# A fused encoder layer on one core: the forget gates' functions at the ends of two pairs, and chained sums in ada's first blocks

## The chip, the cores and the metric

The kernel runs on one NeuronCore of a Trainium2 chip. The metric is the device time of one execution in microseconds. A core has five engines with queues of their own: TensorE (PE, with its weight loads shown as PEld), VectorE (DVE), ScalarE (ACT), GpSimd (POOL) and SyncE (SP). They wait for one another by semaphores. Each engine executes its queue in order, so an instruction that waits holds back all that stand behind it.

## What is computed

One layer of a streaming encoder on x (512 tokens, 1024 channels, float32), with a conditioning vector c. Cut to what the change touches:

```python
mod = silu(c) @ ada_w + ada_b                 # 9 x 1024 columns: shift, scale, gate of three sub-layers
h = rms_norm(x) * (1 + sc1) + sh1             # from the first two of the nine
x = x + 0.5 * g1 * swiglu(h, ...)             # FFN 1: 22 x 128 hidden columns
h = rms_norm(x) * (1 + sc2) + sh2
qa, ka, va, fa, qb, kb, vb, ga, gb = split(h @ mix_w_in)
log_f = log_sigmoid(fa + forget_b)            # 8 heads, 512 tokens
F = cumsum(log_f)                             # branch a: logits get F_t - F_s, causal mask
y_b = attention(qb, kb, vb, relative bias)    # branch b: bias by clipped distance, chunk mask
x = x + g2 * (sigmoid(ga) * (y_a @ wa) + sigmoid(gb) * (y_b @ wb)) @ w_out
x = x + 0.5 * g3 * swiglu(...)                # FFN 2, then a last rms_norm
```

## The kernel before, in words

Every product is made of three float32r matmuls (high x high, high x low, low x high; `three`, lines 1489 to 1491). So each weight unit (1024 columns of 128 rows) is loaded by SyncE's queue, copied to a high half by ScalarE (`prep`, line 616) and subtracted to a low half by VectorE (`prep`, line 945). Activations are stored transposed, channels on the partitions.

**Ada's first blocks.** The 1024 shift and 1024 scale columns of the first sub-layer come in four blocks (b = 0 to 3) of 512 columns, each with eight rows of weights a partition (k = 0 to 7), loaded in two halves (`load_first_block`, line 437). A block's sum over the 1024 channels is made in three parts. GpSimd multiplies and adds rows 0 and 1 (`first_rows`, lines 501 to 510, three instructions a block, into `adasp`). VectorE sums the next rows, up to `ROWS_V[b]` (`first_rows`, lines 1071 to 1085, into `adasc`). TensorE multiplies the last rows, those in `ROWS_PE[b]`, by the conditioning itself (`first_parts`, line 1524), and adds `adasp` and `adasc` over the partitions by products with ones (`first_sums`, line 1512). These are matmuls of one column, and the profile counts each float32 one twice. VectorE adds the parts and the bias (`first_columns`, line 1087), scales two tiles of the normalised input (line 1006), ScalarE makes their high half (line 638), VectorE the low half (line 1011). Then TensorE multiplies these two tiles by the first four weight units (`tiles`, in `first_units`, line 1532). The order of TensorE and VectorE is written out by hand: `first_units` mixes `tiles(u, b)`, `first_parts(b)` and `first_sums(b)`; VectorE's `normed` (line 1014) has the rows of block 3 in two pieces around block 2's tiles. `dummies(n)` (line 1613) issues small bf16 matmuls whose result nothing reads.

**The pairs of heads.** Token mixing has two branches. Branch b (relative bias) goes first: `pairs(0)`, four pairs of heads, then `branch(0)`; `pairs(1)` is branch a (forget gates). A pair has five units: queries, keys, values, two gate units. TensorE makes them, the scores of both heads, the transposes of v, then unit 3 (24 matmuls), the transposes of the first head's probabilities (`turn(0)`, line 1822), half of unit 4, the first head's value products (lines 1837 and 1838), and so on. VectorE adds the bias and finds the largest score (`biased_scores`, line 1344), ScalarE takes the exponentials (line 815), VectorE divides (`normalised`, line 1356). The first two pairs of branch b are straight code, `body(0, True)`; the first has its queries, keys and values already made (`made`).

**The forget gates.** ScalarE makes |f| and a rectified part (lines 912 and 913), then in the first pair `forget_exp` (line 774) and `forget_logs` (line 778): Exp, Ln, Exp on 8 partitions x 512. VectorE's `forget_sums` (line 1285), six instructions, stands at the end of the first pair and ends with the running sum. GpSimd then runs, in its queue's order: `biases_b(0)`, `biases_b(1)`, wait for the running sum, write it to memory (line 591), `biases_a(0)` (four broadcasts, line 549, and four masks, line 555), `biases_b(2)`, `biases_b(3)` (a load, line 536, and a mask, line 540), `biases_a(1)` and on. `bias` is one buffer for a pair of branch b, so `biases_b(i)` also waits until the pair before has added its bias; VectorE's first `biased_scores` of pair i waits for `bias_masked` of that pair.

Of the kernel before, what the change touches and what calls it, by code (L numbers as in the profile page):

```python
# [5 lines left out]
ALU = mybir.AluOpType  # L6
# [3 lines left out]
BF16 = mybir.dt.bfloat16  # L10
ds = bass.ds

P = 128
# [5 lines left out]
def hybrid_block(nc, x, c, ada_w, ada_b, norm_ffn1, ffn1_w_gate, ffn1_w_up, ffn1_w_down,  # L19
# [11 lines left out]
    DT = D // P  # L31
# [55 lines left out]
    C_N1, C_NM, C_N2, C_AB, C_GB = 0, DT, 2 * DT, 3 * DT, 3 * DT + N_MOD * DT  # L87
# [8 lines left out]
    ADA0, ADA1, ADA2 = 4, FT // 2 - 1, DT // 2  # L96
# [1 line left out]

    ROWS_P = 2
    ROWS_PE = ((6, 7), (5, 6, 7), (7,), ())
    ROWS_V = [DT - len(rows) for rows in ROWS_PE]

    N_FIRST = 4
    DUMMIES = 44
# [8 lines left out]
    with ctx:  # L115
# [380 lines left out]
        def _(pool):  # L496
# [4 lines left out]
            def first_rows(b):  # L501
                pool.wait_ge(adas_in[b][0], 32)

                nc.gpsimd.tensor_scalar(adasp[:, b, :], adas[:, b, 0, :], csilu[:, 0:1], None, ALU.mult).then_inc(adasp_step, 1)
                for k in range(1, ROWS_P):
                    scaled = sqx[:, 0:AC] if k % 2 else sqx[:, AC:]
                    pool.wait_ge(adasp_step, (b * ROWS_P + k) * 2 - 1 - b)
                    nc.gpsimd.tensor_scalar(scaled, adas[:, b, k, :], csilu[:, k:k + 1], None, ALU.mult).then_inc(adasp_step, 1)
                    pool.wait_ge(adasp_step, (b * ROWS_P + k) * 2 - b)
                    nc.gpsimd.tensor_tensor(adasp[:, b, :], scaled, adasp[:, b, :], ALU.add).then_inc(adasp_step, 1)  # L510

            def relative_table():
# [89 lines left out]
        def _(act):  # L602
# [168 lines left out]
                half_high(2, 0, range(4, DT))  # L771
                half_high(2, 1, range(DT))

            def forget_exp():
                act.wait_ge(fa_act, 1)
                nc.scalar.activation(fgate[:, 1, :], fgate[:, 0, :], ACT.Exp, scale=-1.0).then_inc(fa_act, 1)

            def forget_logs():

                act.wait_ge(fa_act, 2)  # L780
                nc.scalar.activation(fgate[:, 2, :], fgate[:, 1, :], ACT.Ln, bias=1.0).then_inc(fa_act, 1)
                act.wait_ge(fa_act, 3)
                nc.scalar.activation(fgate[:, 4, :], fgate[:, 2, :], ACT.Exp, scale=-1.0).then_inc(fa_act, 1)

            def pairs(br):
                u0 = U_MIX[br]

                def body(i, first=False):
                    for pp in range(2):
# [11 lines left out]
                                    nc.scalar.activation(dst[head_rows(h ^ other), h, :], bank[head_rows(h), k, :], ACT.Copy,  # L801
                                                         scale=sc).then_inc(qhi, 1)
                        if made:
                            forget_exp()
                            prep(u0, 10, i, k0 + 3)
                        act.wait_ge(unit_done, i * 10 + u0 + k0 + 3)
                        nc.scalar.activation(vT[:, :], bank[:, B_V if made else 0, :], ACT.Copy).then_inc(v_copied, 1)
                        if made:
                            forget_logs()
                        prep(u0, 10, i, k0 + 4)  # L810
                        for h in range(2):
                            for n, t in enumerate(T_ORDER):
# [48 lines left out]
                        gate(1)  # L861
                        out_part(1)
                        out_hi(1)

                if br == 0:
                    body(0, True)
# [63 lines left out]
        def _(dve):  # L930
# [83 lines left out]
            def normed():  # L1014
                every = slice(0, SEQ)
                diagonals(0, slice(0, TT))
                first_rows(0, 4, ROWS_V[0])
                first_prep(0)
                first_prep(1)
                dve.wait_ge(bc_done, 1)  # L1020
                dve.wait_ge(xt_done, DT)
                for b in range(DT // 2):
                    if b in (1, 2):
                        first_rows(b, ROWS_P, ROWS_V[b])
                    if b == 1:
                        first_prep(2)
                        first_prep(3)
                    if b == 2:
                        first_rows(3, ROWS_P, 4)
                    if b == 3:  # L1030
                        first_rows(3, 4, ROWS_V[3])
                    first_columns(b)
                    for d in (2 * b, 2 * b + 1):
                        scaled(0, 0, d, every, B_BC[0])
                    for d in (2 * b, 2 * b + 1):
                        low(0, 0, d, every)
# [33 lines left out]

            def first_rows(b, k0, k1):
                acc = bank[:, B_ACC, :]
                done = sum(n - ROWS_P for n in ROWS_V[:b])
                for k in range(k0, k1):
                    if k == k0 or k % 4 == 0:
                        dve.wait_ge(adas_in[b][k // 4], 32)
                    out = adasc[:, b, :] if k == ROWS_V[b] - 1 else acc
                    if k > ROWS_P or b:
                        dve.wait_ge(adas_step, done + k - ROWS_P)
                    if k == ROWS_P:  # L1080
                        ins = V.tensor_scalar(out, adas[:, b, k, :], csilu[:, k:k + 1], None, ALU.mult)
                    else:
                        ins = V.scalar_tensor_tensor(out=out, in0=adas[:, b, k, :], scalar=csilu[:, k:k + 1],
                                                     in1=acc, op0=ALU.mult, op1=ALU.add)
                    ins.then_inc(adas_step, 1)

            def first_columns(b):

                def pick(t, c0, stride):
                    return t[:, c0:c0 + 2 * stride].rearrange("p (a d) -> p a d", a=2)  # L1090
                if b == 0:
# [4 lines left out]
                done = sum(4 if rows else 3 for rows in ROWS_PE[:b])  # L1096
                V.tensor_tensor(out, sums[:, 0], pick(prm, C_AB, DT)[:, :, 2 * b:2 * b + 2], ALU.add).then_inc(mod_first, 1)
                for s in range(1, 3 if ROWS_PE[b] else 2):
# [206 lines left out]
            def pairs(br):  # L1305
                u0 = U_MIX[br]

                def body(i, first=False):
                    for pp in range(2):
# [15 lines left out]
                            V.tensor_tensor(kHL[head_rows(1 - h), h, :], bank[head_rows(h), 1, :], f32(kHL[head_rows(h), h, :]),  # L1325
                                            ALU.subtract).then_inc(d_free[1], 1)
                        prep(u0, 10, i, k0 + 3)
                        prep(u0, 10, i, k0 + 4)

                        def biased_scores(h):  # L1330
                            for n, t in enumerate(T_ORDER):
# [42 lines left out]

                        biased_scores(0)
                        biased_scores(1)
                        normalised(0)
                        dve.wait_ge(vhi, g * 2 + 2)
                        for e in range(2):
# [8 lines left out]
                        prep(u0, 10, i, k0 + 6)  # L1388
                        out_sum(1)
                        out_lo(1)  # L1390
                        if made:
                            forget_sums()

                if br == 0:
# [46 lines left out]
            first_rows(0, ROWS_P, 4)  # L1441
# [42 lines left out]
        def _(pe):  # L1484
# [26 lines left out]

            def first_sums(b):

                for n in range(2 * AC // P):
                    if n == 0:
                        pe.wait_ge(adasp_step, (b + 1) * (2 * ROWS_P - 1))
                    if n == AC // P:
                        pe.wait_ge(adas_step, sum(n_v - ROWS_P for n_v in ROWS_V[:b + 1]))
# [13 lines left out]
            def first_units():  # L1532
# [10 lines left out]

                dummies(20)
                tiles(0, 0)
                tiles(1, 0)
                first_parts(1)
                first_sums(1)
                tiles(2, 0)
                tiles(3, 0)  # L1550
                tiles(0, 1)
                tiles(1, 1)
                tiles(2, 1)
                first_parts(2)
                first_sums(2)
                tiles(3, 1)
                tiles(0, 2)
                tiles(1, 2)
                first_sums(3)
                tiles(2, 2)  # L1560
                tiles(3, 2)
                for u in range(N_FIRST):
                    tiles(u, 3)

# [48 lines left out]
            def dummies(n):  # L1613

                for _ in range(n):
                    T.matmul(bank[:, B_IDLE, 0:2 * P], ident[:, :].bitcast(BF16)[:, 0:P], ident[:, :].bitcast(BF16), start=True, stop=True)  # L1616

            def spread():
                pe.wait_ge(diag_done, 1)
# [360 lines left out]
```

## Time and profile before

| | us |
|---|---|
| median of 3 runs | 1170.51 (1170.43 to 1171.03) |
| the profiled execution | 1172.53 |
| its span, first to last instruction | 1170.8 |
| TensorE busy | 1154.2 |
| VectorE busy | 625.7 |
| ScalarE busy | 451.4 |
| GpSimd busy | 59.1 |

The profiled execution's own time is 1.7 us more than its span, which is what lies around the instructions. Times in the rows are microseconds from the span's start. In a timeline a row gives start, duration, engine, line of the kernel, operation, tiles written and read, shape and count; the brackets at its end say how long the engine was idle before it and whose work ended that. Matmuls overlap, so their durations are longer than the distance between two starts. In a row of a window, each engine has its busy time and its instructions, and the number after GpSimd's is the granted TensorE clock as a share of 2.4 GHz.

### The profile page before, as it was taken

The page shows a single profiled execution, that of the slowest core. Times are in us where ns is not written, and L with a number is a line of the kernel's source. Part 1 is how long each engine was busy: PE and PEld are TensorE (multiplying, and loading weights), DVE is VectorE, ACT ScalarE, POOL GpSimd, SP SyncE. Part 2 cuts the span into 40 slices and gives each one's busy share as a digit, 9 for nine tenths or more (in the row PEclk, how much of TensorE's full clock was granted, in tenths as well). Part 3 has the DMA queues.
Part 4 walks back from the last instruction along what each step waited for, and adds up shares of the span by engine and source line. Part 5 has one row for each costly group of instructions (what it writes and reads, how often), then busy time and mean ns, then how long its engine had stood idle before and what let it go on. Part 6 is the DMA issues. An engine that isn't in the chain of part 4 may idle for free.

```text
span 1170.8 us, 16224 instructions
## 1 busy us (share of the span) xinstructions
PE 1154.2 (99%) x5734; PEld 977.2 (83%) x5734; DVE 625.7 (53%) x1052; ACT 451.4 (39%) x709; POOL 59.1 (5%) x86
## 2 busy tenths in 40 slices
PE   8999999999999998999999999999999999999998
PEld 7788888888888997888888888899888888888887
DVE  4766666666555666765555666756333333333332
ACT  4132232233222355655555666543332222322232
POOL 3301000000000000200000110000000000000000
PEclk9799999999999998999999999999999999999999
DMA  9567666556555413533244442241333333333331
GB/s 313 157 198 245 196 202 211 168 178 224 172 169 164 111 56 90 136 91 90 72 114 96 115 118 87 84 125 47 108 90 94 103 90 101 96 85 99 99 112 73
DMA packets 221149, 151.45 MB, mean 129 GB/s; under 512 B 5078, under 2 KB 202916, under 8 KB 221108
## 3 DMA queue, kind: packets, MB, share of 16 engines
q1 hardware_dynamic: 217108, 138.76, 39.4%
q0 software_dynamic: 3280, 9.79, 3.1%
q10 hardware_dynamic: 720, 2.36, 0.5%
q8 instruction: 25, 0.41, 0.1%
q14 instruction: 16, 0.13, 0.0%
HBM read 148.73 MB, written 4.52 MB: 131 GB/s over the span
## 4 chain that ended last, share of the span: by engine, by line
PE 93%; DVE 2%; issue 2%; DMA 1%; ACT 1%; ACTq 0%; DVEq 0%; POOLq 0%; POOL 0%; SPq 0%
PE bank L1489 28%; PE bank L1491 28%; PE bank L1490 28%; PE bank L1822 2%; PE bank L1838 1%; PE bank L1837 1%; PE bank L1815 1%; PE bank L1810 1%; DMA xin<-in_x_dram 1%; DMA raw<-in_ffn_w_gate_dram 1%; PE bank L1520 1%; DVE hL L1011 1%; PE bank L1616 0%; PE bank L1529 0%; DVE tmp L1006 0%
## 5 line engine op out<-in xcount | busy, mean ns | idle before, releaser
L1489 PE MATMUL bank<-hH,wH 128*128 128x512 f32 (+1 forms) x1072 | 414.3, 386 | 2.6 <-DVE hL L1011 2.2
L1490 PE MATMUL bank<-hL,wH 128*128 128x512 f32 (+1 forms) x1072 | 410.2, 383 | 0.0
L1491 PE MATMUL bank<-hH,wL 128*128 128x512 f32 (+1 forms) x1072 | 410.1, 383 | 0.0
L616 ACT ACTIVATE wH<-raw 128x1024 fp32r<-128x1024 f32 (+1 forms) x169 | 176.1, 1042 | 503.7 <-PE bank L1491 503.7
L945 DVE TENSOR_TENSOR wL<-raw,wH 128x1024 fp32r<-128x1024 f32 (+1 forms) x169 | 203.2, 1202 | 286.1 <-ACT wH L616 285.5
L1489 PEld LDWEIGHTS bank<-hH,wH 128*128 128x128 f32 x1072 | 202.6, 189 | 43.4 <-issue 4.4
L1491 PEld LDWEIGHTS bank<-hH,wL 128*128 128x128 f32 x1072 | 202.3, 189 | 39.5
L1490 PEld LDWEIGHTS bank<-hL,wH 128*128 128x128 f32 x1072 | 202.5, 189 | 38.3
L1489 PE MATMUL bank<-actH,wH 128*128 128x512 f32 (+1 forms) x332 | 126.9, 382 | 0.0
L1491 PE MATMUL bank<-actH,wL 128*128 128x512 f32 (+1 forms) x332 | 126.6, 381 | 0.0
L1490 PE MATMUL bank<-actL,wH 128*128 128x512 f32 (+1 forms) x332 | 126.6, 381 | 0.0
L957 DVE SCALAR_TENSOR_TENSOR adac<-adaw,csilu,adac 128x512 f32<-128x512 f32 (+1 forms) x98 | 73.6, 751 | 2.6
L1122 DVE TENSOR_TENSOR adac<-adac,bank 128x512 f32<-128x512 f32 x44 | 30.2, 687 | 80.6 <-PE bank L1491 79.9
L1489 PEld LDWEIGHTS bank<-actH,wH 128*128 128x128 f32 x332 | 62.4, 188 | 12.2 <-issue 0.2
L1491 PEld LDWEIGHTS bank<-actH,wL 128*128 128x128 f32 x332 | 62.4, 188 | 12.0
L1490 PEld LDWEIGHTS bank<-actL,wH 128*128 128x128 f32 x332 | 62.4, 188 | 12.0
L815 ACT ACTIVATE prob<-prob,negmax 128x512 f32<-128x512 f32 (+1 forms) x64 | 35.1, 552 | 16.2 <-DVE negmax L1344 16.2
L562 POOL TENSOR_TENSOR nrm<-nrm,mhalf 128x2 f32<-128x2 f32 (+1 forms) x7 | 5.2, 750 | 598.5 <-DVE nrm L981 598.5
L1163 DVE SCALAR_TENSOR_TENSOR xT<-bank,gres,xT 128x512 f32 (+1 forms) x19 | 14.3, 751 | 31.6 <-PE bank L1491 31.0
L1126 DVE TENSOR_TENSOR actL<-adac,actH 128x512 f32 (+1 forms) x44 | 30.1, 684 | 0.2
L660 ACT ACTIVATE actH<-adac 128x512 f32 (+1 forms) x44 | 27.1, 616 | 1.8 <-DVE adac L1122 1.8
L1361 DVE TENSOR_TENSOR ptL<-bank,ptH 128x512 fp32r<-128x512 f32 (+1 forms) x32 | 25.6, 818 | 0.5 <-ACT ptH L836 0.3
(204 smaller groups left out, 1200.3 us busy)
## 6 DMA issues: line engine op xcount, KB each, us to landing
adaw<-in_ada_w_dram SPq DMA_DIRECT2D x28, 1024.0 KB, 5.9
raw<-in_ffn_w_gate_dram SPq DMA_DIRECT2D x43, 512.0 KB, 3.7
raw<-in_ffn_w_up_dram SPq DMA_DIRECT2D x43, 512.0 KB, 3.7
raw<-in_mix_w_in_dram SPq DMA_DIRECT2D x41, 512.0 KB, 3.7
raw<-in_ffn_w_down_dram SPq DMA_DIRECT2D x32, 512.0 KB, 3.7
adas<-in_ada_w_dram SPq DMA_DIRECT2D x16, 512.0 KB, 8.0
raw<-in_ffn_w_down_dram SPq DMA_DIRECT2D x16, 384.0 KB, 3.4
raw<-in_mix_w_out_dram SPq DMA_DIRECT2D x8, 512.0 KB, 3.7
```

Source lines behind the costliest of these rows:

```text
L616: nc.scalar.activation(wH[s][:, :n * P], raw[s][:, :n * P], ACT.Copy).then_inc(hi_done, 1)
L660: nc.scalar.activation(actH[:, ds(i * 2 + j, 1), :], pr[:, j:j + 1, :], ACT.Copy).then_inc(actH_done[n], 1)
L815: nc.scalar.activation(prob[:, h, T_OFF[t]:T_OFF[t] + w], prob[:, h, T_OFF[t]:T_OFF[t] + w], ACT.Exp, scale=-1.0, bias=negmax[:, h, t:t + ...
L945: V.tensor_tensor(wL[s][:, :n * P], raw[s][:, :n * P], f32(wH[s][:, :n * P]), ALU.subtract).then_inc(lo_done, 1)
L957: ins = V.scalar_tensor_tensor(out=acc, in0=adaw[:, q, r:r + 1, :width], scalar=csilu[:, k:k + 1], in1=acc, op0=ALU.mult, op1=ALU.add)
L1122: V.tensor_tensor(pr[:, j, :], sg[:, j, :], bank[:, 2 * j + 1, :], ALU.mult).then_inc(prod_done[n][j], 1)
L1126: V.tensor_tensor(actL[:, ds(i * 2 + j, 1), :], pr[:, j:j + 1, :], f32(actH[:, ds(i * 2 + j, 1), :]), ALU.subtract).then_inc(actL_done[n], 1)
L1361: V.tensor_tensor(ptL[:, cols], bank[:, S_BANK[h]:S_BANK[h] + 3, :].rearrange("p a b -> p (a b)")[:, cols], f32(ptH[:, cols]), ALU.subtrac ...
L1489: T.matmul(o, a[0], b[0], start=start, stop=False)
L1490: T.matmul(o, a[0], b[1], start=False, stop=False)
L1491: return T.matmul(o, a[1], b[0], start=False, stop=stop)
L1822: ins = T.transpose(flat(hh)[:, J_OFF[j] + (t - j) * P:J_OFF[j] + (t - j + 1) * P], prob[:, hh, T_OFF[t] + j * P:T_OFF[t] + (j + 1) * P], ...
```

## The change

ScalarE: the Exp and Ln of the forget gates (`forget_log`) are issued at the end of the first pair, the last Exp (`forget_exp`) at the end of the second. VectorE: `forget_sums` is issued at the end of the second pair instead of the first, and in the first pair the low half of unit 4 behind both heads' `biased_scores` instead of ahead of them. GpSimd's queue has the same order.

Ada's first blocks: `ROWS_PE` gives VectorE five rows in block 1 and four in block 3 (they were three and six) and TensorE one and two (three and none). In blocks 2 and 3 (`CHAINED`) VectorE's first row adds to GpSimd's sum, for which it waits, and TensorE adds only VectorE's. TensorE's order is another, and 26 dummies are added in three places; dummies now write the upper 256 columns of a bank.

```diff
-    ROWS_P = 2
-    ROWS_PE = ((6, 7), (5, 6, 7), (7,), ())
+    ROWS_P = (2, 2, 2, 2)
+
+    CHAINED = (2, 3)
+    ROWS_PE = ((6, 7), (7,), (7,), (6, 7))
     ROWS_V = [DT - len(rows) for rows in ROWS_PE]
+    SUMS = [(() if b in CHAINED else (0,)) + (1,) + ((2,) if rows else ()) for b, rows in enumerate(ROWS_PE)]
+    STEPS_P = [sum(2 * r - 1 for r in ROWS_P[:b]) for b in range(ADA0 + 1)]
+    STEPS_V = [sum(v - r for r, v in zip(ROWS_P[:b], ROWS_V)) for b in range(ADA0 + 1)]
...
-            def forget_exp():
+            def forget_log():
                 act.wait_ge(fa_act, 1)
                 nc.scalar.activation(fgate[:, 1, :], fgate[:, 0, :], ACT.Exp, scale=-1.0).then_inc(fa_act, 1)
-
-            def forget_logs():
-
                 act.wait_ge(fa_act, 2)
                 nc.scalar.activation(fgate[:, 2, :], fgate[:, 1, :], ACT.Ln, bias=1.0).then_inc(fa_act, 1)
+
+            def forget_exp():
                 act.wait_ge(fa_act, 3)
                 nc.scalar.activation(fgate[:, 4, :], fgate[:, 2, :], ACT.Exp, scale=-1.0).then_inc(fa_act, 1)
...
                         if made:
-                            forget_exp()
                             prep(u0, 10, i, k0 + 3)
                         act.wait_ge(unit_done, i * 10 + u0 + k0 + 3)
                         nc.scalar.activation(vT[:, :], bank[:, B_V if made else 0, :], ACT.Copy).then_inc(v_copied, 1)
-                        if made:
-                            forget_logs()
                         prep(u0, 10, i, k0 + 4)
...
                         out_hi(1)
+                        if first:
+                            (forget_log, forget_exp)[pp]()
...
-                    if k == ROWS_P:
+                    if k == ROWS_P[b] and b in CHAINED:
+                        dve.wait_ge(adasp_step, STEPS_P[b + 1])
+                        ins = V.scalar_tensor_tensor(out=out, in0=adas[:, b, k, :], scalar=csilu[:, k:k + 1],
+                                                     in1=adasp[:, b, :], op0=ALU.mult, op1=ALU.add)
+                    elif k == ROWS_P[b]:
...
                         prep(u0, 10, i, k0 + 3)
-                        prep(u0, 10, i, k0 + 4)
+                        if not made:
+                            prep(u0, 10, i, k0 + 4)
...
                         biased_scores(1)
+                        if made:
+                            prep(u0, 10, i, k0 + 4)
...
-                        if made:
+                        if first and pp == 1:
                             forget_sums()
...
-                for n in range(2 * AC // P):
+                for n in range(AC // P if b in CHAINED else 0, 2 * AC // P):
...
                 dummies(20)
                 tiles(0, 0)
+                first_parts(1)
                 tiles(1, 0)
-                first_parts(1)
+                dummies(10)
                 first_sums(1)
                 tiles(2, 0)
                 tiles(3, 0)
                 tiles(0, 1)
                 tiles(1, 1)
+                first_parts(2)
                 tiles(2, 1)
-                first_parts(2)
+                tiles(3, 1)
                 first_sums(2)
-                tiles(3, 1)
+                first_parts(3)
+                dummies(10, B_ADA_START[3])
                 tiles(0, 2)
                 tiles(1, 2)
+                tiles(2, 2)
                 first_sums(3)
-                tiles(2, 2)
                 tiles(3, 2)
+                dummies(6, B_ADA_START[2])
                 for u in range(N_FIRST):
                     tiles(u, 3)
```

## Rows read from the trace of the kernel before

**Rows 1.** The page, busy time of the engines

```profile
PE 1154.2 (99%) x5734; PEld 977.2 (83%) x5734; DVE 625.7 (53%) x1052; ACT 451.4 (39%) x709; POOL 59.1 (5%) x86
```

**Rows 2.** Busy time by window: us, PE, PEld, DVE, ACT, POOL, PEclk, DMA, GB/s

```profile
44.55:51.38 6.83, 6.18 (x15) 4.33 (x16) 6.40 (x12) 1.38 (x2) 0.00 (x0) 0.50 0.00 0
62.00:76.00 14.00, 14.00 (x63) 11.58 (x63) 8.60 (x12) 4.74 (x7) 0.00 (x0) 1.00 0.82 264
447.31:454.14 6.83, 5.87 (x19) 5.09 (x20) 5.79 (x14) 4.74 (x12) 0.89 (x2) 0.50 0.26 77
```

**Rows 3.** ScalarE's timeline in the first pair of branch b

```profile
439.21 1.28 ACT L783 ACT_TABLE_LOAD   x1
440.50 0.63 ACT L783 ACTIVATE fgate<-fgate 8x512 f32<-8x512 f32 x1
...
444.12 0.72 ACT L815 ACTIVATE prob<-prob,negmax 128x512 f32<-128x512 f32 x1 [2.03 <-DVE negmax L1344]
```

**Rows 4.** VectorE's timeline in the first pair

```profile
442.12 1.23 DVE L945 TENSOR_TENSOR wL<-raw,wH 128x1024 fp32r<-128x1024 f32 x1 [4.45 <-ACT wH L616]
```

**Rows 5.** TensorE's timeline in the first and in the second pair

```profile
448.27 2.39 PE L1822 MATMUL bank<-ident,prob 128*128 128x128 f32 x10 [3.22 <-DVE prob L1356]
...
454.95 0.39 PE L1837 MATMUL bank<-ptH,vHL 128*128 128x512 f32 x1
...
486.10 1.25 PE L1822 MATMUL bank<-ident,prob 128*128 128x128 f32 x10
...
489.94 0.39 PE L1837 MATMUL bank<-ptH,vHL 128*128 128x512 f32 x1
```

**Rows 6.** Timelines of VectorE, GpSimd and TensorE in ada's third and fourth blocks

```profile
42.44 0.76 DVE L1083 SCALAR_TENSOR_TENSOR bank<-adas,csilu,bank 128x512 f32<-128x512 f32 x1
44.58 0.16 DVE L1097 TENSOR_TENSOR mod<-bank,prm 128x4 f32<-128x4 f32 x1 [1.39 <-PE bank L1520]
...
54.18 0.16 DVE L1097 TENSOR_TENSOR mod<-bank,prm 128x4 f32<-128x4 f32 x1 [2.83 <-PE bank L1520]
...
41.63 1.27 POOL L510 TENSOR_TENSOR adasp<-sqx,adasp 128x512 f32<-128x512 f32 x1
...
47.81 0.77 PE L1489 MATMUL bank<-hH,wH 128*128 128x512 f32 x1 [0.65 <-DVE hL L1011]
...
53.11 1.03 PE L1520 MATMUL bank<-ones,adasc 128*128 128x1 f32 x8
...
57.44 0.47 PE L1489 MATMUL bank<-hH,wH 128*128 128x512 f32 x1 [0.41 <-DVE hL L1011]
```

**Rows 7.** ScalarE's timeline at the start of the second pair

```profile
467.04 1.06 ACT L616 ACTIVATE wH<-raw 128x1024 fp32r<-128x1024 f32 x1 [3.03 <-PE bank L1491]
```

**Rows 8.** GpSimd's timeline, from the gates' sum to the biases

```profile
469.56 0.56 POOL L591 DMA_DIRECT2D negF_d<-fgate  x1 [17.91 <-DVE fgate L1302]
471.65 2.84 POOL L549 DMA_DIRECT2D biasA<-negF_d  x4 [1.53 <-DMA negF_d<-fgate]
482.23 1.48 POOL L555 TENSOR_SCALAR_AFFINE_SELECT biasA<-biasA 128x256 f32<-128x256 f32 x4 [7.74 <-DMA biasA<-negF_d]
...
488.53 0.29 POOL L540 TENSOR_SCALAR_AFFINE_SELECT bias<-bias 128x128 f32<-128x128 f32 x1 [3.38 <-DMA bias<-relb_d]
...
619.56 1.48 POOL L555 TENSOR_SCALAR_AFFINE_SELECT biasA<-biasA 128x256 f32<-128x256 f32 x4 [5.60 <-DMA biasA<-negF_d]
```

**Rows 9.** VectorE's timeline, ends of two pairs and the third pair

```profile
464.76 0.41 DVE L1289 TENSOR_SCALAR fgate<-fgate 8x512 f32<-8x512 f32 x1
...
499.02 0.69 DVE L1372 TENSOR_TENSOR oL<-osum,oH 64x512 fp32r<-64x512 f32 x1 [0.69 <-ACT oH L848]
...
515.68 0.69 DVE L1344 CUSTOM_DVE_ANT_0 prob<-bank,bias 128x512 f32<-128x512 f32 x1
...
519.24 1.50 DVE L1356 TENSOR_SCALAR prob<-prob,rinv 128x512 f32<-128x512 f32 x4
```

**Rows 10.** TensorE's timeline in the third pair

```profile
521.08 1.25 PE L1822 MATMUL bank<-ident,prob 128*128 128x128 f32 x10
```

More of the change, by code:

```diff
@@ L504, in first_rows @@
                 nc.gpsimd.tensor_scalar(adasp[:, b, :], adas[:, b, 0, :], csilu[:, 0:1], None, ALU.mult).then_inc(adasp_step, 1)
-                for k in range(1, ROWS_P):
+                for k in range(1, ROWS_P[b]):
                     scaled = sqx[:, 0:AC] if k % 2 else sqx[:, AC:]
-                    pool.wait_ge(adasp_step, (b * ROWS_P + k) * 2 - 1 - b)
+                    pool.wait_ge(adasp_step, STEPS_P[b] + 2 * k - 1)
                     nc.gpsimd.tensor_scalar(scaled, adas[:, b, k, :], csilu[:, k:k + 1], None, ALU.mult).then_inc(adasp_step, 1)
-                    pool.wait_ge(adasp_step, (b * ROWS_P + k) * 2 - b)
+                    pool.wait_ge(adasp_step, STEPS_P[b] + 2 * k)
                     nc.gpsimd.tensor_tensor(adasp[:, b, :], scaled, adasp[:, b, :], ALU.add).then_inc(adasp_step, 1)
@@ L1023, in normed @@
                     if b in (1, 2):
-                        first_rows(b, ROWS_P, ROWS_V[b])
+                        first_rows(b, ROWS_P[b], ROWS_V[b])
                     if b == 1:
@@ L1028, in normed @@
                     if b == 2:
-                        first_rows(3, ROWS_P, 4)
+                        first_rows(3, ROWS_P[3], 4)
                     if b == 3:
@@ L1072, in first_rows @@
                 acc = bank[:, B_ACC, :]
-                done = sum(n - ROWS_P for n in ROWS_V[:b])
                 for k in range(k0, k1):
@@ L1077, in first_rows @@
                     out = adasc[:, b, :] if k == ROWS_V[b] - 1 else acc
-                    if k > ROWS_P or b:
-                        dve.wait_ge(adas_step, done + k - ROWS_P)
-                    if k == ROWS_P:
+                    if k > ROWS_P[b] or b:
+                        dve.wait_ge(adas_step, STEPS_V[b] + k - ROWS_P[b])
+                    if k == ROWS_P[b] and b in CHAINED:
[3 more added lines that the diff above has]
+                    elif k == ROWS_P[b]:
                         ins = V.tensor_scalar(out, adas[:, b, k, :], csilu[:, k:k + 1], None, ALU.mult)
@@ L1095, in first_columns @@
                 sums = bank[:, B_ADA_START[b], 0:12].rearrange("p (s a d) -> p s a d", s=3, a=2)
-                done = sum(4 if rows else 3 for rows in ROWS_PE[:b])
-                V.tensor_tensor(out, sums[:, 0], pick(prm, C_AB, DT)[:, :, 2 * b:2 * b + 2], ALU.add).then_inc(mod_first, 1)
-                for s in range(1, 3 if ROWS_PE[b] else 2):
+                done = sum(len(terms) + 1 for terms in SUMS[:b])
+                V.tensor_tensor(out, sums[:, SUMS[b][0]], pick(prm, C_AB, DT)[:, :, 2 * b:2 * b + 2], ALU.add).then_inc(mod_first, 1)
+                for s in SUMS[b][1:]:
                     done += 1
@@ L1440, in _ @@
             mean_squares(0, slice(0, TT))
-            first_rows(0, ROWS_P, 4)
+            first_rows(0, ROWS_P[0], 4)
             normed()
@@ L1512, in first_sums @@
             def first_sums(b):
-                for n in range(2 * AC // P):
+                for n in range(AC // P if b in CHAINED else 0, 2 * AC // P):
                     if n == 0:
-                        pe.wait_ge(adasp_step, (b + 1) * (2 * ROWS_P - 1))
+                        pe.wait_ge(adasp_step, STEPS_P[b + 1])
                     if n == AC // P:
-                        pe.wait_ge(adas_step, sum(n_v - ROWS_P for n_v in ROWS_V[:b + 1]))
+                        pe.wait_ge(adas_step, STEPS_V[b + 1])
                     cols = slice(n % (AC // P) * P, (n % (AC // P) + 1) * P)
@@ L1611, in last_sums, with dummies @@
                 return ins
-            def dummies(n):
+            def dummies(n, b=B_IDLE):
                 for _ in range(n):
-                    T.matmul(bank[:, B_IDLE, 0:2 * P], ident[:, :].bitcast(BF16)[:, 0:P], ident[:, :].bitcast(BF16), start=True, stop=True)
+                    T.matmul(bank[:, b, 2 * P:], ident[:, :].bitcast(BF16)[:, 0:P], ident[:, :].bitcast(BF16), start=True, stop=True)
             def spread():
```

## The prediction

> **What bounds the kernel now.** I read the page first, then the windows, then the timelines of the two places that the change touches. TensorE is busy 99% of the span [rows 1], so a change pays only where TensorE sits idle, where it runs at its lower clock, or where it does work that can be dropped. The windows [rows 2] give the price of the clock: at 2.4 GHz (granted 1.00) it issues 62 full-width matmuls in 14 us (the row counts 63, with those cut at the window's edges), 0.226 us each; two stretches of 6.83 us are granted 0.50, which is 1.2 GHz. One is in ada's first blocks, one in the first pair of heads.
>
> *The first pair.* Between the queries and the exponentials, ScalarE loads three tables (Exp, Ln, Exp) for the forget gates; a load takes 1.28 us [rows 3]. Only then comes the conversion for which VectorE waits 4.45 us before its subtraction, and the score reductions stand behind that subtraction [rows 4]. TensorE runs out of work at 445.05 and waits 3.22 us for the probabilities [rows 5], then goes on at half clock: from the first transpose to the first value product it takes 6.68 us (448.27 to 454.95), in the second pair 3.84 us (486.10 to 489.94) [rows 5].
>
> *Ada's first blocks.* The chain goes back and forth: VectorE sums rows, TensorE adds over partitions, VectorE makes the columns and normalises two tiles, TensorE multiplies them. The third block's columns start at 44.58, TensorE's tiles at 47.81, the fourth block's columns at 54.18 and its tiles at 57.44 [rows 6].
>
> **The change, part by part.** The sum is made against the profiled execution, 1172.53 us (span 1170.8 and 1.7 around it), which stands 2.0 us above the median of the runs, 1170.51. I take 2.0 off at the end.
>
> *1. Gates' functions leave the first pair.* VectorE was free at 437.67 (442.12 less 4.45) and TensorE's last unit before the stall, 24 matmuls or 5.4 us ending at 445.05, began at 439.6, so all scores are there by then. Reductions that begin about 437.7, the 4.9 us from the end of that subtraction to the first transpose (442.12 + 1.23 = 443.35 to 448.27), and 1.2 us for the subtraction, which now stands behind the reductions, give 443.8: before 445.05. The stall goes, and with it 448.27 - 444.9 = 3.4 us. One Exp load stays, before the first exponential; ScalarE has 2.03 us of idle there [rows 3], which covers 1.28. Without the stall the clock has no reason to fall: 3.84 in place of 6.68, -2.8. Together -6.2; bounds -3.4 (the clock falls all the same) and -6.3. Nothing is late next, since the second pair has the same order and no stall.
>
> *2. Exp and Ln at the end of the first pair.* 0.63 + 1.28 + 0.63 us of ScalarE before its next conversion, in front of which it idles 3.03 us [rows 7]: 0. If that cover were gone, the conversion would be late, and its matmuls come two units afterwards, so still 0. The Exp table has to come back in pair two, before an exponential with the same kind of 2 us idle; 0, or 0.6 if the load stands behind the wait instead of before it. The Trainium skill (ScalarE: Activation LUTs, "What ACT_TABLE_LOAD costs") states a drain of about 1.4 us on top of each load. By that rule the first load would overrun its idle time by 0.9 us, the second its own by 0.6, and the sum would be some 0.3 us higher; the trace disagrees, its load being followed by the next function within 0.02 us.
>
> *3. The gates' sum moves to the end of pair two.* On VectorE it costs 4.5 us of its own time, as before, under TensorE's units: 0. But **what stands behind it on GpSimd moves too.** GpSimd's queue is: send the sum to memory, broadcast it into the first branch-a bias, mask it, and only then load and mask the bias of the third pair of branch b. Before, this ran under pair two: send at 469.56, broadcast 471.65, masks 482.23, third pair's bias landed and masked by 488.8 [rows 8], long before its use at 515.68 [rows 9]. Now the sum starts when pair two's last subtraction ends, 499.02 + 0.69 = 499.7, and takes the 4.8 us that it took from 464.76 to 469.56: the send goes at 504.5. Then 2.1 to the broadcast, 10.6 to the masks, 1.5 for them, 4.1 for the third pair's bias (0.7 to issue, as 2.84 for four, and 3.4 to land) and 0.3 for its mask: ready at 523.1. VectorE wants it at 515.68, so it waits 7.4 us at the head of its queue, with every reduction, division and low half of pair three behind it; ScalarE's exponentials wait for VectorE, and TensorE for both. TensorE had 0.34 us in hand (probabilities done at 519.24 + 1.50 = 520.74, transposes at 521.08) [rows 9, 10]. Its stall is **7.1 us**. Lower bound: the quickest later broadcast waited 5.60 in place of 7.74 [rows 8], so 5.0; upper 7.4.
>
> *4. The clock after that stall.* TensorE idle for 7 us will fall to 1.2 GHz; 3.2 us of idle did it in pair one. There the stretch cost 2.8. Bounds 0 and 3.1 (all 6.83 us of such a stretch under matmuls 0.41 apart, 15 in 6.18 us [rows 2]). Part of a stretch can lie under the idle time itself, so I take +2.2.
>
> *5. Ada's first blocks.* I count the blocks from one. VectorE sums five rows in the second block instead of three and four in the fourth instead of six; in the third and fourth it starts from GpSimd's sum. TensorE loses 16 of the small matmuls (0.11 us each, from eight in 0.9 [rows 6]) and gains 26 dummies, which lie where it would wait. The second block's columns come about 1 us sooner, since TensorE has two rows fewer to multiply ahead of its sums. But the third block's do not: VectorE takes the fourth block's first rows ahead of them, and those now begin only when GpSimd's last add ends, 41.63 + 1.27 = 42.9 [rows 6], two rows of 0.76 later it is 44.5, against 44.58. So TensorE again starts the third block's tiles at 47.8. After them come 18 matmuls in place of 12 before the fourth sums, and 8 small ones in place of 16: +1.4 and -0.9, +0.5 in all if the clock is at 0.50 there as before. If it stays at 1.00, 18 matmuls take 4.1 and the sums 0.9, the columns come at 52.8 and not 54.18: -1.4. TensorE still has a hole of several us before 47.8 with only short work in it, so I take +0.5. A chained row has both operands in SBUF; I price it as the other rows, 0.76. Wider bounds, since where the clock falls moves with everything: down, -3, the half of the stretch at 0.50 that matmuls at 0.41 in place of 0.226 lose in it (15 x 0.18 = 2.8 [rows 2]); up, +2, a few of the 18 matmuls more at half clock than now.
>
> Sum: -6.2 + 7.1 + 2.2 + 0.5 = **+3.6**, 1176.1 for the profiled execution, **1174.1** for the median.
>
> **The rivals.**
> *A. Faster: the third pair's bias is not late enough to matter.* Its place is GpSimd's queue between the gates' sum and that bias, its price the 9.3 us of steps 3 and 4, and it decides where wait and clock together stay under 6.2 less what ada brings. With the quickest broadcast and a clock that holds, 5.0 and 0: -6.2 + 5.0 - 1.4 = -2.6, 1167.9. If the bias were not late at all it would be 1164.8. For it: broadcasts differ by 2 us. Against: the queue's order is fixed, and each stage has its row. 0.13.
> *B. A draw: ada holds its clock.* The dummies sit just where TensorE was at 0.50; with -1.4 there and 5.9 + 1.5 in pair three the sum is -0.2, 1170.3; with the full 7.1 + 2.2 it is +1.7. For it: the first fall, after a long run of small matmuls, has dummies now. Against: the hole before 47.8. 0.24.
> *C. Slower still:* ada's reordering costs 2 us in place of 0.5, the Exp load in pair two stands behind the wait (0.6), and the half clock after the stall costs its full 3.1 in place of 2.2: +6.6, 1177.1. For it: each is within the bounds above. Against: it needs them all. 0.13.
> *D. The gates' move does nothing*, because TensorE's stall in pair one has another cause (the branch-b bias, or scores): then +9.8. Against: VectorE's wait names ScalarE's conversion. 0.02.
>
> **How the numbers follow.** My forecast has 0.48, A 0.13, B 0.24, C 0.13, D 0.02. The range goes from A's better part to past C, 1168 to 1178.5. Faster by over 0.2% (2.3 us, about what a measurement of this kernel can tell from no change) is A, 0.13; within it is B, 0.24; slower is the rest, 0.63.
>
> **What would show it.** In pair one: no wait of TensorE for the probabilities, granted clock 1.00 after it. In pair three: VectorE idle some 7 us before its first reduction, put down to GpSimd's mask; TensorE waiting about 7 us for the probabilities; 0.50 after. GpSimd's load of the third pair's bias after its four masks for branch a, not before pair three begins. In ada: GpSimd's add ending at 42.9 with VectorE's chained row right behind it, third block's tiles at about 47.8, fourth's at 56 to 58. The forecast is wrong if pair three shows a wait under 4 us, or if ada's tiles move by more than 2.

## The result, and the profile after

The changed kernel takes 1175.13 us, median of 6 runs (1174.78 to 1176.24), against 1170.22 us of the kernel before, measured beside it (1169.76 to 1171.03). The ratio is 1.0045, with a 95% interval of 1.0033 to 1.0058: it is slower, by 4.9 us. I had forecast 1174.1, 3.6 us over the kernel before. The profiled execution took 1175.29 us, its span is 1173.6, so between the two profiled executions the difference is only 2.8.

The waits of TensorE, for the whole span. The columns are: in all, how often, the longest.

```profile
PE bank L1835 <- DVE prob L1363: 6.7, 1, 6.7
...
PE bank L1498 <- DVE hL L1014: 3.5, 7, 1.1
```

The 3.2 us for the probabilities in the first pair are gone, and one of 6.7 has come. Where it lies, and what it costs behind itself, is in TensorE's timeline: the first pair's transposes and first value product, then the third pair's.

```profile
445.35 1.25 PE L1835 MATMUL bank<-ident,prob 128*128 128x128 f32 x10
...
449.19 0.39 PE L1850 MATMUL bank<-ptH,vHL 128*128 128x512 f32 x1
...
522.13 1.11 PE L1835 MATMUL bank<-ident,prob 128*128 128x128 f32 x4 [6.67 <-DVE prob L1363]
...
527.69 0.39 PE L1850 MATMUL bank<-ptH,vHL 128*128 128x512 f32 x1
```

In the first pair the way from transposes to values is now 3.84 us (6.68 in [rows 5]). In the third pair the transposes start after 6.67 us of idle time, and the same way takes 5.56 us, 1.7 more than at full clock. The third pair's transposes had no wait in front of them before [rows 10]. The granted clock says the same (windows of the changed kernel; the columns are those of [rows 2]): 1.00 in the first pair, 0.77 on average over the third pair's stall and what follows. In the window of ada's blocks that stood at 0.50 before it is 0.75. That window is not the only one with half clock in ada's blocks: from 20 to 60 us the granted clock is 0.79 in the profile of before and 0.87 in that of the changed kernel.

```profile
44.55:51.38 6.83, 6.59 (x37) 5.53 (x37) 5.00 (x10) 1.38 (x2) 0.00 (x0) 0.75 0.00 0
...
445.00:452.00 7.00, 7.00 (x46) 6.21 (x45) 5.04 (x11) 4.25 (x7) 0.29 (x1) 1.00 0.48 140
515.00:530.00 15.00, 8.33 (x44) 7.17 (x42) 10.18 (x40) 8.75 (x24) 1.29 (x3) 0.77 0.22 65
```

ScalarE's timeline shows where the loads of tables went. The first is ahead of the first pair's first exponential, the second and the Ln at the first pair's end, the third ahead of the second pair's first exponential.

```profile
438.67 1.28 ACT L816 ACT_TABLE_LOAD   x1
439.96 0.72 ACT L816 ACTIVATE prob<-prob,negmax 128x512 f32<-128x512 f32 x1
...
458.91 1.28 ACT L783 ACT_TABLE_LOAD   x1
460.20 0.63 ACT L783 ACTIVATE fgate<-fgate 8x512 f32<-8x512 f32 x1
461.26 1.06 ACT L621 ACTIVATE wH<-raw 128x1024 fp32r<-128x1024 f32 x1 [0.43 <-PE bank L1500]
...
473.64 1.28 ACT L816 ACT_TABLE_LOAD   x1
475.66 0.72 ACT L816 ACTIVATE prob<-prob,negmax 128x512 f32<-128x512 f32 x1 [0.73 <-DVE negmax L1351]
```

The load at 473.64 stands ahead of the wait, not behind it: it starts while VectorE's first score is still to come, and 0.73 us of idle time is left after it. The conversion at 461.26 still finds 0.43 us of idle time before it. After the first two loads the next function starts 0.01 us later than the load ends, after the third as soon as its data is there. The drain that the Trainium skill (ScalarE: Activation LUTs, "What ACT_TABLE_LOAD costs") states beside a load does not show here either.

GpSimd's timeline, to be laid beside [rows 8], is the one that makes the loss:

```profile
498.76 0.56 POOL L596 DMA_DIRECT2D negF_d<-fgate  x1 [51.97 <-DVE fgate L1308]
500.85 2.85 POOL L554 DMA_DIRECT2D biasA<-negF_d  x4 [1.53 <-DMA negF_d<-fgate]
510.82 1.48 POOL L560 TENSOR_SCALAR_AFFINE_SELECT biasA<-biasA 128x256 f32<-128x256 f32 x4 [7.12 <-DMA biasA<-negF_d]
512.25 0.72 POOL L541 DMA_DIRECT2D bias<-relb_d  x1
516.59 0.29 POOL L545 TENSOR_SCALAR_AFFINE_SELECT bias<-bias 128x128 f32<-128x128 f32 x1 [3.62 <-DMA bias<-relb_d]
```

And VectorE's, the last subtraction of pair two and the small instruction ahead of pair three's first reduction:

```profile
493.24 0.69 DVE L1379 TENSOR_TENSOR oL<-osum,oH 64x512 fp32r<-64x512 f32 x1 [0.69 <-ACT oH L849]
...
516.94 0.06 DVE L939 MEMSET spare<- 128x1 f32 x1 [7.08 <-POOL bias L545]
```

The gates' sum starts after 493.24 + 0.69, the send goes at 498.76, the broadcasts' masks at 510.82, and only then GpSimd turns to the third pair's bias, which is masked at 516.88. VectorE has stood 7.08 us at the head of its queue, and the wait names GpSimd's mask.

Ada's blocks: VectorE's rows, GpSimd's last add, TensorE's dummies and tiles, beside [rows 6].

```profile
43.37 0.76 DVE L1084 SCALAR_TENSOR_TENSOR bank<-adas,csilu,adasp 128x512 f32<-128x512 f32 x1 [1.61 <-POOL adasp L515]
...
44.83 0.16 DVE L1103 TENSOR_TENSOR mod<-bank,prm 128x4 f32<-128x4 f32 x1
...
54.60 0.16 DVE L1103 TENSOR_TENSOR mod<-bank,prm 128x4 f32<-128x4 f32 x1 [4.78 <-PE bank L1529]
...
41.94 1.29 POOL L515 TENSOR_TENSOR adasp<-sqx,adasp 128x512 f32<-128x512 f32 x1
...
46.36 1.25 PE L1629 MATMUL bank<-ident 128*128 128x256 bf16 x10
47.85 0.77 PE L1498 MATMUL bank<-hH,wH 128*128 128x512 f32 x1 [0.24 <-DVE hL L1014]
...
57.85 0.47 PE L1498 MATMUL bank<-hH,wH 128*128 128x512 f32 x1 [1.11 <-DVE hL L1014]
```

VectorE waits 1.61 us for GpSimd's add, which ends at 43.23, and the third block's columns come at 44.83 against 44.58 before. The ten dummies at 46.36 stand where the kernel before had tiles of the second block at half clock and then 0.65 us of idle time; those tiles now come earlier, and 0.24 us of idle time is left. The third block's tiles start 0.04 us later than before, and the fourth block's at 57.85 against 57.44.

### The profile page after: what moved, and what is told of

Read it like the earlier page. It is cut to its first block, busy times and chain, and to the rows that moved or that the text cites. A ratio compares the mean times of both kernels' runs of the same rounds, so it can differ in the third digit from the quotient of the medians.

```text
span 1173.6 us, 16243 instructions
## 1 busy us (share of the span) xinstructions
PE 1151.8 (98%) x5744; PEld 974.6 (83%) x5744; DVE 626.1 (53%) x1051; ACT 451.9 (39%) x709; POOL 58.3 (5%) x86
## 4 chain that ended last, share of the span: by engine, by line
PE 84%; issue 6%; DMA 3%; DVE 2%; SPq 2%; ACT 1%; POOL 1%; DVEq 0%; POOLq 0%; ACTq 0%
PE bank L1498 26%; PE bank L1500 26%; PE bank L1499 26%; PE bank L1835 1%; SPq L446 1%; DMA adas<-in_ada_w_dram 1%; DMA bias<-relb_d 1%; DMA raw<-in_ffn_w_gate_dram 1%; PE bank L1851 1%; DMA biasA<-negF_d 1%; PE bank L1850 1%; SPq L465 1%; PE bank L1823 1%; PE bank L1828 1%; DVE hL L1014 1%
## 5 line engine op out<-in xcount | busy, mean ns | idle before, releaser
L1835 PE MATMUL bank<-ident,prob 128*128 128x128 f32 x160 | 21.4, 283 | 6.7 <-DVE prob L1363 6.7
```

What stands on the lines that cost most here:

```text
L1835: ins = T.transpose(flat(hh)[:, J_OFF[j] + (t - j) * P:J_OFF[j] + (t - j + 1) * P], prob[:, hh, T_OFF[t] + j * P:T_OFF[t] + (j + 1) * P], ...
```

## The experiments

The theory, called Q below: the loss is made by GpSimd's queue, in which the third pair's bias stands behind the gates' sum; all else gives the gain of the first pair and little more. The rival R: ada's new order makes it. Beside them stand D (the dummies hold the clock up in ada's blocks; not the prediction's rival D) and N (the order of VectorE and GpSimd sets when ada's tiles start), and F on ScalarE. Times are medians, each beside the kernel before on the same chip: e1 to e4 are one set, e5 to e8 another, e9 and e10 a third. The runs of the kernel before lie further apart there than in the first measurement (1167.8 to 1173.4 in the set of 28), so medians and ratios can differ by over 1 us; I give both where it matters, go by what the traces show, and call no difference under 1 us real.

| run | what it is | us | before | ratio, 95% |
|---|---|---|---|---|
| e1 | the change, third bias ahead | 1167.31 | 1170.19 | 0.9973 (0.9963 to 0.9984) |
| e2 | gates' part alone | 1174.27 | 1170.19 | 1.0028 (1.0016 to 1.0040) |
| e3 | ada's part alone | 1172.21 | 1170.19 | 1.0006 (0.9994 to 1.0018) |
| e4 | gates' part, third bias ahead | 1165.49 | 1170.19 | 0.9952 (0.9938 to 0.9967) |
| e5 | the gates' sum late, nothing else | 1178.74 | 1170.33 | 1.0068 (1.0046 to 1.0090) |
| e6 | e1 without the 26 dummies | 1169.14 | 1170.33 | 0.9985 (0.9972 to 0.9997) |
| e7 | e1, fourth block's rows behind | 1164.84 | 1170.33 | 0.9948 (0.9929 to 0.9967) |
| e8 | e4, VectorE's order as before | 1165.17 | 1170.33 | 0.9944 (0.9926 to 0.9963) |
| e9 | e7, TensorE's sums sooner | 1163.60 | 1169.87 | 0.9951 (0.9939 to 0.9964) |
| e10 | e7 again | 1165.02 | 1169.87 | 0.9966 (0.9953 to 0.9979) |

**e1: the third pair's bias ahead.** Two lines of GpSimd's queue change places.

```diff
                     biases_b(0)
                     biases_b(1)
+                    biases_b(2)
                     pool.wait_ge(negF_done, 1)
...
                     biases_a(0)
-                    biases_b(2)
                     biases_b(3)
```

> The changed kernel, with GpSimd's load of the third pair's bias put ahead of its wait for the gates' sum. Theory Q (that queue makes the loss): the 6.7 us wait of TensorE in the third pair goes and the half clock after it too (2 us), so 8 to 9.5 us under the changed kernel: about 1166. Rival R (ada's new order makes the loss, the wait in pair three is paid back elsewhere): it stays within 2 us of the changed kernel, 1173 to 1175.

1167.31 us, 7.8 under the changed kernel's 1175.13 (8.4 by the two ratios), and 0.27% under before. The waits of TensorE, all of them:

```profile
PE bank L1629 <- POOL ident L503: 3.9, 1, 3.9
PE bank L1498 <- DVE hL L1014: 3.3, 6, 1.1
PE bank L1498 <- DVE hL L1433: 0.4, 1, 0.4
PE bank L1608 <- DVE work L1001: 0.2, 1, 0.2
```

There is none for the probabilities left, in any pair. Q holds, R falls: R left no room for more than 2 us.

**e2 and e4: the gates' part alone, without and with that move.** Both are the kernel before with the ScalarE and VectorE lines of the pairs changed as in the diff; e4 has e1's edit too.

> The kernel before with the gates' part of the change alone (functions, sum and the low half of unit 4 moved; ada as before). Q: 6.2 us won in the first pair, 6.7 of wait and about 2 of half clock lost in the third: +2.5 to +3.5 over before, 1173 to 1174. R: at or below before, 1164 to 1170.

> The kernel before with the gates' part and with the third pair's bias ahead of the wait for the gates' sum. Q: the whole 6.2 us of the first pair, 1164. R says the same here; what tells is e2 against it, 9 us by Q and 0 by R.

e2 took 1174.27, 4.1 over before by the medians and 3.3 by the ratio; e4 1165.49, 4.7 under it. Ada's blocks are those of before in both, so 8.8 us hang on the place of one load in GpSimd's queue. It is the cleanest of the comparisons: one set, one edit. The one wait of e2 for the probabilities:

```profile
PE bank L1823 <- DVE prob L1355: 6.2, 1, 6.2
```

e4's gain, 4.7 by the medians and 5.6 by the ratio, is less than the 6.2 of the first pair. That is taken up below.

**e3: ada's part alone.** The changed kernel with the pairs as they were.

> The changed kernel with the gates' part undone: ada's blocks alone. Q: within 1.5 us of before, 1169.5 to 1172, since the fourth block's tiles start where they did (57.85 against 57.44 in the profiles). R: 4 us or more over before, 1174 to 1176.

1172.21 against 1170.19; the ratio, 1.0006, is within its interval of none. Between nothing and 2 us of loss, which leaves R no room for the 4 it asked for. The number at which Q had its own upper end, 1172, is just missed. A second comparison is sharper. e1 and e4 have the same gates' part and the same place of the bias, and differ only in ada's blocks: 1167.31 (11 runs, 1166.30 to 1168.50) against 1165.49 (6 runs, 1164.32 to 1166.63). So ada's part costs some 1.8 us there by the medians, 2.5 by the ratios. It gains nothing, and it costs more than the 0.5 that I had.

**e5: the gates' sum late, nothing else.**

```diff
-                        if made:
+                        if first and pp == 1:
                             forget_sums()
```

> The kernel before with VectorE's gates' sum moved to the end of the second pair and nothing else: ScalarE's functions stay in the first pair. Theory Q (the sum's place holds up GpSimd's queue): both stalls are there, 3.2 us in pair one and 6 to 7 in pair three with half clock after it, 8 to 9 us over before: 1178 to 1179. A rival, F (it is ScalarE's Exp at the end of pair two and its table load that make pair three late): no stall in pair three, 1170.

1178.74, 8.4 over before: the price of the late bias by itself, as Q had it. ScalarE's three functions are back in the first pair, and still the third pair stalls, so F falls. TensorE's timeline, first pair and third:

```profile
446.71 2.40 PE L1822 MATMUL bank<-ident,prob 128*128 128x128 f32 x10 [3.22 <-DVE prob L1356]
...
452.02 0.39 PE L1837 MATMUL bank<-ptH,vHL 128*128 128x512 f32 x1
...
524.49 2.40 PE L1822 MATMUL bank<-ident,prob 128*128 128x128 f32 x10 [6.20 <-DVE prob L1356]
```

The first pair's stall is the same 3.22 us as in the kernel before, but the way from transposes to values is 5.31 us here, not 6.68: the clock fell for a shorter time behind the very same wait.

Ada's blocks, whose code is that of before, also got another clock in this execution. The window 20 to 60 us in the profile of before, then in e5's that window and the one that stood at 0.50 before, and the start of the fourth block's tiles:

```profile
20.00:60.00 40.00, 38.94 (x191) 32.28 (x191) 28.61 (x49) 8.49 (x11) 13.79 (x9) 0.79 0.65 190
...
20.00:60.00 40.00, 36.70 (x201) 31.43 (x201) 29.63 (x52) 10.09 (x13) 13.78 (x9) 0.91 0.65 192
44.55:51.38 6.83, 5.08 (x26) 3.99 (x26) 6.37 (x12) 1.38 (x2) 0.00 (x0) 1.00 0.00 0
...
55.82 0.47 PE L1489 MATMUL bank<-hH,wH 128*128 128x512 f32 x1 [0.41 <-DVE hL L1011]
```

The fourth block's tiles start at 55.82 and not at 57.44, and TensorE comes to the first pair's stall 1.56 us sooner, at 443.49 (446.71 less 3.22) where it was 445.05. So the two stretches of half clock that the prediction starts from are those of one execution of the kernel before, not of each.

**e8: the functions without VectorE's reorder.** e4, but the subtraction for unit 4 of the first pair ahead of the reductions again.

> The gates' part with the bias ahead (1165.5), but VectorE's subtraction for unit 4 of the first pair back ahead of the reductions, as in all other pairs. Q: the functions alone made the stall of pair one, since the subtraction is then ready at 439.5 and the reductions end by 443: no wait of TensorE, 1165 to 1166. The rival (the reorder made the gain): a wait of 2 to 3 us in pair one, 1168 to 1170.

1165.17, the same as e4's 1165.49 within the noise. VectorE's subtraction and first reduction, and TensorE's transposes:

```profile
436.88 1.23 DVE L943 TENSOR_TENSOR wL<-raw,wH 128x1024 fp32r<-128x1024 f32 x1 [1.73 <-ACT wH L616]
...
438.15 0.69 DVE L1342 CUSTOM_DVE_ANT_0 prob<-bank,bias 128x512 f32<-128x512 f32 x1
...
443.55 1.25 PE L1820 MATMUL bank<-ident,prob 128*128 128x128 f32 x10
```

The subtraction is out of the way at 438.11, and the transposes have no wait in front of them. The gain is the functions'; the reorder adds nothing once they are gone.

**e6: no dummies.** e1 with the three calls of `dummies` that the change adds taken out.

> The changed kernel with the third pair's bias ahead, less the 26 dummies. D (the dummies hold the clock up in ada's blocks): more stretches at 0.50 in the first 60 us and 1.5 to 3 us over the same kernel with them, 1168.5 to 1170. N (the order of VectorE and GpSimd sets the tiles, dummies lie in waits): within 1 us, 1166.5 to 1168.

1169.14 against 1167.31 for e1, in two sets of runs, ratios 0.9985 and 0.9973: within D's range of 1168.5 to 1170, but the intervals overlap (0.9972 to 0.9984). The wait of TensorE for its tiles, and the stretch from 24 to 60 us of this run:

```profile
PE bank L1498 <- DVE hL L1014: 8.5, 7, 3.1
...
24.00:60.00 36.00, 29.31 (x142) 23.66 (x143) 24.39 (x41) 6.46 (x9) 12.32 (x9) 0.91 0.60 174
```

The same stretch of e1:

```profile
24.00:60.00 36.00, 33.84 (x186) 27.54 (x185) 25.86 (x42) 8.50 (x12) 12.27 (x9) 0.92 0.60 173
```

The granted clock is nearly the same, 0.91 and 0.92; what differs is that TensorE is busy 29.3 us without the dummies and 33.8 with them, and waits 8.5 us for low halves in place of 3.3. D's first sign, more half clock in the first 60 us, is not there. But the half clock lies elsewhere. The window 46.4 to 53.3 us, over the third block's tiles, first without the dummies and then in e1:

```profile
46.40:53.30 6.90, 5.89 (x14) 4.67 (x15) 2.83 (x4) 0.73 (x2) 0.00 (x0) 0.51 0.00 0
...
46.40:53.30 6.90, 6.90 (x32) 5.51 (x29) 3.04 (x5) 0.97 (x2) 0.00 (x0) 0.75 0.00 0
```

Without them these tiles run at 0.51 and the fourth block's start at 58.57, with them at 0.75 and at 57.25. That fits D. As e5 shows that the clock here differs by execution of one and the same code, one profile of each does not settle it: D stays open.

**e7: the fourth block's rows behind the third block's tiles.** The wait for GpSimd's last add leaves the path of the third block's columns.

```diff
-                    if b == 2:
-                        first_rows(3, ROWS_P[3], 4)
                     if b == 3:
-                        first_rows(3, 4, ROWS_V[3])
+                        first_rows(3, ROWS_P[3], ROWS_V[3])
```

> The changed kernel with the third pair's bias ahead, and on VectorE the fourth block's first two rows behind the third block's tiles and not ahead of them. N (the wait for GpSimd's last add, 1.6 us, and two rows of 0.8 hold up the third block's tiles): its columns come 1.5 to 3 us sooner and the fourth block's tiles up to 2 us sooner, 1165 to 1166.5. The rival (TensorE's order and clock set it): within 0.7 us of 1167.3.

1164.84, and 1165.02 when it was run again (e10), 2.3 to 2.5 under e1. VectorE's third columns, chained row and fourth columns, then TensorE's tiles of the third and fourth blocks:

```profile
42.73 0.16 DVE L1101 TENSOR_TENSOR mod<-bank,prm 128x4 f32<-128x4 f32 x1 [1.70 <-PE bank L1527]
...
46.18 0.76 DVE L1082 SCALAR_TENSOR_TENSOR bank<-adas,csilu,adasp 128x512 f32<-128x512 f32 x1
...
52.16 0.16 DVE L1101 TENSOR_TENSOR mod<-bank,prm 128x4 f32<-128x4 f32 x1 [2.79 <-PE bank L1527]
...
45.75 0.77 PE L1496 MATMUL bank<-hH,wH 128*128 128x512 f32 x1
...
55.42 0.47 PE L1496 MATMUL bank<-hH,wH 128*128 128x512 f32 x1 [1.11 <-DVE hL L1014]
```

The columns come at 42.73 where they came at 44.83 (44.62 in e1's profile), the chained row at 46.18 has no wait any more, and the fourth block's tiles start at 55.42 (57.25 in e1's profile, 57.85 in the changed kernel's). N holds. e7 and e1 were run in two sets, but e10 gives e7's number again in a third.

**e9 and e10: TensorE's sums sooner.** `first_sums(2)` ahead of `tiles(3, 1)`, `first_sums(3)` ahead of `tiles(2, 2)`; e10 is e7 unchanged.

> e7 with the third block's sums one unit sooner on TensorE (ahead of the fourth weight unit's tiles) and the fourth block's sums ahead of the third unit's tiles, as in the kernel before. N (the chain of VectorE and TensorE sets the tiles): 0.7 us sooner at the third block's columns and 0.5 to 1.4 more at the fourth's, 1 to 2 us under e7. The rival (the small matmuls bring the clock down where they stand now, and TensorE has to wait as long): within 0.7 us of e7.

> e7 unchanged, beside e9 on the same chip: 1164.8 again, within 0.8 us, and 5 to 6 us under before.

1163.60 and 1165.02: 1.4 us by the medians, with intervals that overlap, so the gain is likely and not certain. e10 repeats e7 as expected; under before it is by 4.9 us, just short of the 5 to 6. VectorE's columns of the third and fourth blocks in e9:

```profile
43.68 0.16 DVE L1101 TENSOR_TENSOR mod<-bank,prm 128x4 f32<-128x4 f32 x1 [1.73 <-PE bank L1527]
...
51.48 0.16 DVE L1101 TENSOR_TENSOR mod<-bank,prm 128x4 f32<-128x4 f32 x1 [1.17 <-PE bank L1527]
```

The third block's are not sooner than in e7 (43.68 against 42.73), though that was the first half of what I expected; the fourth's are, by 0.7 us (51.48 against 52.16). The granted clock differs between these executions too: from 20 to 28 us it is 0.57 in e9 and 0.79 in e10, and from 44 to 60 us 1.00 and 0.89, so the two profiles don't tell the order's share from the clock's. e9 has the lowest median of all, 0.49% under the kernel before by its ratio, and is under both kernels. The ratios of e7 and e8 in their own set (0.9948 and 0.9944) are as low, so these three are not ranked.

## Why the prediction was right, and where its sizes were off

**Step 1, the first pair:** as forecast in what happens. No wait, full clock, 3.84 us for the way to the values. e8 adds that the functions alone do it. The -6.2 is right against the execution that I started from: the profiles of before and e4, with the same 0.79 from 20 to 60 us, are 5.9 apart (1172.53 and 1166.63). Over many executions it is -4.7 to -5.6 (e4).

**Step 2, Exp and Ln:** 0 was right. The load in pair two stands ahead of its wait, so the 0.6 us of rival C did not arise, and the 0.3 us by the rule of the Trainium skill (ScalarE: Activation LUTs, "What ACT_TABLE_LOAD costs") have no row either.

**Step 3, GpSimd's queue:** this makes the loss, shown by e1, e2 against e4, and e5. I had 7.4 us for VectorE's wait and 7.1 for TensorE's; they are 7.08 and 6.67. The broadcasts waited 7.12 us, between my two rows, and the bias 3.62.

**Step 4, the clock:** +2.2 forecast, 5.56 - 3.84 = 1.7 in the profile. Steps 3 and 4 together are 9.3 in the forecast, 8.8 in e2 against e4.

**Step 5, ada:** +0.5 forecast, 57.85 - 57.44 = 0.4 in the profiles. GpSimd's add held VectorE as described. I had thought that the second block's columns would come 1 us sooner; nothing depended on it. But 0.4 is the distance to one execution of before. The old order's fourth tiles start at 57.44 to 57.70 in three profiles (before, e2, e4), with 0.50 to 0.52 in the window 44.55 to 51.38, and at 55.82 and 56.03 in two (e5, e8), with 1.00 there. The new order's start at 57.25 to 58.25 in all three that have it whole (e1, the changed kernel, e3). So the new order costs little where the old one gets half clock, and 1.4 us or more where it does not; by the medians of e1 and e4 it costs 1.8.

By the profiles the sum is -3.2 - 2.8 + 6.7 + 1.7 + 0.4 = +2.8, which is the difference of the two executions (1175.29 - 1172.53). The runs without a profile say +4.9. What was mis-sized is the base: the -2.8 of the first pair's half clock and the +0.5 of ada's blocks were both worked out against one execution and then carried over to the median. The prediction even says that this execution stood 2.0 us over the median, and takes the 2.0 off at the end, as if the excess lay outside of what the change touches. It lay inside, in part at least.

The granted clock over the whole span was taken for every execution, and it sorts the 28 of before in e1's set into three groups:

| granted clock | executions | us |
|---|---|---|
| 0.988 | 9 | 1172.8 to 1173.4 |
| 0.991 to 0.993 | 7 | 1170.1 to 1171.0 |
| 0.994 to 0.995 | 12 | 1167.8 to 1170.2 |

The profile that I started from had 0.988, as in the first of the three. The changed kernel's six executions have 0.991 or 0.992 and lie within 1.5 us. None of the kernel before's executions in the other two groups was profiled, so where they save their time is not shown directly. But e5, with the same code up to the first pair's values, shows both places: 1.56 us ahead of the stall and 1.37 behind it (6.68 less 5.31), 2.9 in all.

By the runs without a profile the terms are -4.7 (e4), +8.8 (e2 against e4) and +1.8 (e1 against e4), +5.9 in all, where +4.9 was measured; a distance of 1 us between sets is within what they can tell. The forecast had -6.2, +9.3 and +0.5. So the wait and its cause were right, and that the total came within 1.3 us is luck in part: pair one was too good by some 1.5 us and ada by some 1.3, while the queue was too dear by 0.5 and the runs themselves don't add up by 1.0. How the shortfall divides between pair one and ada is not settled, since by the ratios pair one is -5.6 and ada +2.5, or +0.7 by e3.

Rival A's case of a bias that is not late at all is what e1 made true by an edit. The prediction put that at 1164.8; it came out at 1167.31, 2.5 us above, and that is the same error in pair one and ada. (A's -2.6, for a quicker broadcast, lies near e1's -2.9 only by chance.) B, the clock held in ada's blocks, came true by half: the granted clock from 20 to 60 us is 0.87 where it was 0.79, but the third block's columns, and so the tiles, were not earlier. Of C, ada's cost of 2 us nearly came, the other two parts did not. D, a stall in pair one with another cause, fell: the stall is gone.

## What to carry to other kernels

When a step moves to a later place on one engine, read the queue of every engine that waits for it to the end: the loss here was a load that had nothing to do with the moved step and only stood behind it. Put loads that can go early ahead of waits for results that come late. And take the price of a half clock from more than one execution; compare its granted clock with that of the other executions first.

## What I had not expected of the hardware

The same 3.22 us of idle time on TensorE was followed by 2.8 us of loss in one execution (before) and 1.5 in another (e5). In one set of 28 runs the kernel before took from 1167.84 to 1173.44 us, and the granted clock went with it, from 0.995 down to 0.988; in the first set of 6 it took only 1169.76 to 1171.03.

In these traces low halves of VectorE, which read both operands from SBUF, took longer where GpSimd's add ran beside them: VectorE's timeline in the changed kernel has two low halves with GpSimd's add beside them, and two without.

```profile
35.42 2.44 DVE L1014 SCALAR_TENSOR_TENSOR hL<-tmp,mod,hH 128x512 fp32r<-128x512 f32 x2
...
46.95 1.42 DVE L1014 SCALAR_TENSOR_TENSOR hL<-tmp,mod,hH 128x512 fp32r<-128x512 f32 x2
...
35.59 1.72 POOL L515 TENSOR_TENSOR adasp<-sqx,adasp 128x512 f32<-128x512 f32 x1
```

The first two took 2.44 us, the last two 1.42; GpSimd's add of the third block ran from 35.59 for 1.72 us, against 1.27 to 1.29 for the others. In e7, where these low halves came 1.5 us sooner, the two took 1.85. No run was made for this alone, so it is a reading of rows.
